# Scaling one half of each expert output block on VectorE, behind the weight splits

## The reference

```python
scores = sigmoid(x @ router_w)                     # 8 of 64 experts for each token, in 4 of 8 groups
w = take_along_axis(scores, top_idx, 1)
w = w / sum(w) * 2.5
def block_fn(acc, inp):                            # blocks of 128 rows, all of one expert
    rows, wts, e = inp
    yb = (silu(x[rows] @ w1[e]) * (x[rows] @ w3[e])) @ w2[e] * wts[:, None]
    return acc.at[rows].add(yb), None
ffn = routed[:N] + (silu(x @ sw1) * (x @ sw3)) @ sw2
x = layernorm(2 ** 0.25 * x + ffn)
```

## Time and profile before

| | |
|---|---|
| median of three runs | 2590.1 us |
| the profiled execution's own time | 2590.1 us |
| its span | 2588.2 us |
| TensorE clock granted, mean over the span | 0.933 |
| busy, of the span: PE, DVE, ACT, POOL | 88%, 48%, 34%, 24% |
| steps of the loop over experts between 1560 and 2515 us | 102 |

### The profile page before, as it was taken

How to read it: one execution, slowest core, us unless ns; L and a number is a source line. 1 busy time by engine, 2 the same in 40 slices (tenths; PEclk the granted TensorE clock), 3 DMA queues, 4 the chain that set the end, 5 groups by cost and what they waited for, 6 DMA issues and landing times.

```text
span 2588.2 us, 33805 instructions
## 1 busy us (share of the span) xinstructions
PE 2285.1 (88%) x8956; PEld 1519.7 (59%) x8957; DVE 1254.3 (48%) x2042; ACT 891.9 (34%) x1157; POOL 611.9 (24%) x412
## 2 busy tenths in 40 slices
PE   8994878999998999999891649999999999999980
PEld 3463554555554544444451538888887888888870
DVE  6365741333333411111337217767687676666647
ACT  1042103020101101000111117767686676666641
POOL 1000000212121100001000663444444444444432
PEclk9997969999999999999895769999999999999995
DMA  3101001000000011114522129999999999999954
GB/s 143 41 19 39 1 9 58 32 33 32 16 8 25 25 41 36 37 36 156 209 98 84 49 60 293 353 352 321 307 353 352 320 363 308 281 305 331 318 135 194
DMA packets 87770, 399.57 MB, mean 154 GB/s; under 512 B 15506, under 2 KB 15763, under 8 KB 61715
## 3 DMA queue, kind: packets, MB, share of 16 engines
q1 hardware_dynamic: 52546, 278.40, 28.2%
q0 software_dynamic: 35184, 120.67, 18.3%
HBM read 322.67 MB, written 75.18 MB: 154 GB/s over the span
## 4 chain that ended last, share of the span: by engine, by line
PE 61%; DVE 4%; DMA 3%; issue 2%; another core or an unknown queue 2%; ACT 1%; POOL 0%; POOLq 0%; ACTq 0%; SPq 0%; DVEq 0%
PE ps L621 33%; PE ps L1276 10%; PE ps L1284 5%; PE ps L615 4%; PE ps L576 3%; PE ps L1138 2%; DMA ffn_rows<-sig 1%; PE ps L647 1%; PE ps L1312 1%; DVE fr L956 1%; DMA wts<-in_experts 1%; PE ps L594 1%; DVE fst L958 0%; PE ps L587 0%
## 5 line engine op out<-in xcount | busy, mean ns | idle before, releaser
L621 PE MATMUL ps<-wts,xgT 128*128 x2616 | 628.6, 396 | 2.0 <-issue 1.9
L621 PEld LDWEIGHTS ps<-wts,xgT 128*128 128x128 f32 x2616 | 485.9, 189 | 102.4 <-issue 3.0
L882 DVE TENSOR_TENSOR wts<-wts (+1 forms) x195 | 444.2, 2291 | 139.6 <-ACT wts L697 78.1
L621 PE MATMUL ps<-wts,hTs 128*128 x1296 | 320.5, 394 | 23.4 <-issue 23.0
L1276 PE MATMUL ps<-xT,ring 128*128 128x512 f32 x768 | 334.7, 593 | 0.0
L540 POOL DMA_INDIRECT ffn_rows<-yo,sx x108 | 213.5, 1977 | 474.6 <-ACT yo L736 455.3
L1138 PE MATMUL ps<-xT,ring 128*128 128x512 f32 x704 | 311.4, 599 | 6.1 <-DMA ring<-in_w_in 6.1
L621 PEld LDWEIGHTS ps<-wts,hTs 128*128 128x128 f32 x1296 | 244.9, 189 | 80.6 <-issue 31.1
L692 ACT ACTIVATE wts<-wts (+1 forms) x130 | 242.9, 1929 | 41.3 <-DMA btab<-block_table 34.7
L1276 PEld LDWEIGHTS ps<-xT,ring 128*128 128x128 f32 x768 | 145.2, 190 | 178.9 <-issue 178.9
L522 POOL DMA_INDIRECT xg<-x_rows,ix x112 | 212.6, 1898 | 107.8 <-DVE ix L906 95.7
(11 more groups left out here) (358 smaller groups left out, 2301.1 us busy)
## 6 DMA issues: line engine op xcount, KB each, us to landing
wts<-in_experts SPq DMA_DIRECT2D x195, 1024.0 KB
ring<-in_w_in SPq DMA_DIRECT2D x52, 512.0 KB, 3.3
bring<-in_w_branch SPq DMA_DIRECT2D x24, 256.0 KB, 2.6
ffn_rows<-sig POOLq DMA_DIRECT2D x9, 512.0 KB
xT<-in_xT SPq DMA_DIRECT2D x4, 1024.0 KB, 9.3
wout<-in_w_out SPq DMA_DIRECT2D x1, 4096.0 KB, 12.2
N<-in_x SPq DMA_DIRECT2D x8, 512.0 KB, 3.6
x_rows<-N SPq DMA_DIRECT2D x8, 512.0 KB, 2.7
```

The costliest lines, as they stand in the source:

```text
L621: ins = mm(o, left(x), slot_cols(s, w, slice(c0, c0 + HALF)), start=first and n == 0, stop=last and n == 2)
L882: tt(w, w.bitcast(F32), hi, ALU.subtract).then_inc(done, 1)
```

## The change

The two halves of an output block no longer both belong to ACT. ACT scales the first (`ps[6]`) as before. DVE scales the second (`ps[7]`), as the last instruction of its step. The two copies `sx` and `wx`, with their wait for the add of two blocks before, move from ahead of the second part of the splits to behind it. The semaphores `e_y[0]`, `e_y[1]` become `e_ya`, `e_yd`, and PE waits for both ahead of the first half of its product.

```diff
@@ tail_pe
+                    pe.wait_ge(e_ya, i * 2 + u + ONE)
+                    pe.wait_ge(e_yd, i * 2 + u + ONE)
                     for h in range(2):
-                        pe.wait_ge(e_y[h], i * 2 + u + ONE)
@@ tail_act
                     act.wait_ge(e_Y, i * 2 + (u + 1) + ONE)
                     act.wait_ge(e_wx, i * 4 + (2 * u + 2))
-                    for h in range(2):
-                        A(yo[:, u, h * HALF:(h + 1) * HALF], ps[6 + h][:], ACT.Copy, scale=wx[:, u:u + 1]).then_inc(e_y[h], 1)
+                    A(yo[:, u, 0:HALF], ps[6][:], ACT.Copy, scale=wx[:, u:u + 1]).then_inc(e_ya, 1)
@@ tail_dve, block_step
                 hid(1 - u, i * 2 + (u + 2), i * 2 + u)
-                dve.wait_ge(e_sc[u], i * 16 + SC0[u])
-                dve.sem_inc(d_go, 1)
-                V.tensor_copy(sx[:, u:u + 1], slt[:, bass.ds(b, 1), 0:1].rearrange("p o w -> p (o w)")).then_inc(e_wx, 1)
-                V.tensor_copy(wx[:, u:u + 1], sltf[:, bass.ds(b, 1), 1:2].rearrange("p o w -> p (o w)")).then_inc(e_wx, 1)
                 with dve.If(first > 0):
                     split13(o, s, 1)
                 o, s, first = rows[u]
                 with dve.If(first > 0):
                     split2(o, s)
+                dve.wait_ge(e_sc[u], i * 16 + SC0[u])
+                dve.sem_inc(d_go, 1)
+                V.tensor_copy(sx[:, u:u + 1], slt[:, bass.ds(b, 1), 0:1].rearrange("p o w -> p (o w)")).then_inc(e_wx, 1)
+                V.tensor_copy(wx[:, u:u + 1], sltf[:, bass.ds(b, 1), 1:2].rearrange("p o w -> p (o w)")).then_inc(e_wx, 1)
+                dve.wait_ge(e_Y, i * 2 + (u + 1) + ONE)
+                dve.wait_ge(e_wx, i * 4 + (2 * u + 2))
+                ts(yo[:, u, HALF:D], ps[7][:], wx[:, u:u + 1], None, ALU.mult).then_inc(e_yd, 1)
```

More of the change, by code:

```diff
@@ L357, in build @@
         e_wx = sem("row_weight_ready")
-        e_y = [sem(f"output_half_scaled{i}") for i in range(2)]
+        e_ya = sem("output_half_act")
+        e_yd = sem("output_half_dve")
         e_sc = [sem(f"rows_adding{i}") for i in range(2)]
@@ L536, in add_rows @@
                 pool.wait_ge(e_sc[u], i * 16 + SC0[u])
-                pool.wait_ge(e_y[0], b + (1 + ONE))
-                pool.wait_ge(e_y[1], b + (1 + ONE))
+                pool.wait_ge(e_ya, b + (1 + ONE))
+                pool.wait_ge(e_yd, b + (1 + ONE))
                 pool.sem_inc(p_go, 1)
@@ L1374, in _ @@
             ch = Chain(act, s_act)
-            for one in (h_ev, *e_y, e_hTe):
+            for one in (h_ev, e_ya, e_hTe):
                 act.sem_inc(one, ONE)
@@ L1543, in _ @@
             ch = Chain(dve, s_dve)
-            for one in (h_o, h_qF, g_mix, e_hTl, e_hm):
+            for one in (h_o, h_qF, g_mix, e_yd, e_hTl, e_hm):
                 dve.sem_inc(one, ONE)
```

## The result

| | before | after |
|---|---|---|
| median (lowest to highest) of four runs | 2590.5 us (2590.0 to 2591.1) | 2660.0 us (2656.0 to 2662.8) |
| profiled execution, its span | 2590.1, 2588.2 | 2654.1, 2652.0 |
| granted clock over the span | 0.933 | 0.934 |
| busy, of the span: PE, DVE, ACT, POOL | 88%, 48%, 34%, 24% | 87%, 50%, 31%, 20% |

The kernel became slower, by a ratio of 1.0267 [1.0249, 1.0285]: 69.5 us. The direction and the place were as forecast. The size was not: +18.6 was expected, and 2660.0 lies far outside the range of 2598 to 2626.

A forecast was written before the change was run, and what follows sets the result against it. PE was taken to bound the expert loop at 9.31 us a step. Stalls 21.2, clock 4.8, late weights -6.8 and ACT's shorter end -0.6 sum to +18.6 on 2590.1: 2608.7 us, range 2598 to 2626.

The forecast's parts named there:

- The bound: In the expert loop PE sets the pace, 9.31 us a step, with 1.45 us of slack for `hm`.
- The ring: ACT's scaling waits for `wx` behind DVE's splits, and DVE's `hm` waits for ACT: 11.57 us against PE's 9.31.
- Its legs: Stretches between ACT's scaling, `hm`, DVE's splits and the copies: 6.27 us to `hm`, 5.30 back to the scaling.
- a run: Consecutive loop steps that each bring a new expert; from n = 3 on it costs 0.9 + 2.26(n-3) us.
- no change: Rival: DVE runs ahead, so ACT finds `wx` early enough; -0.6 to +5 us, about 2592; chance 0.07.
- a gain: Rival: in the shared expert's blocks POOL's add comes about 0.6 us sooner, moving the scatters; 2582 us; chance 0.03.
- The ring is longer than its legs: Rival: DVE's second half pays its branches in full, PE's product also waits for low hidden; +35 us, 2625; chance 0.20.
- the walk: Step-by-step count of lateness and PE stalls through steps with new experts and those behind them; 21.2 us in all.
- y: Time from PE's start of a step to ACT's scaling: 0.28 us before, forecast to reach 4.64.
- POOL's gather behind it: The next gather stands behind POOL's add, which waits for both halves; taken up two steps later, so put at nothing.
- The clock: PE's granted clock falls behind the last stall in runs of four (two) and six: 3 x 1.6 = 4.8 us.
- The weights' credit: Late weights in the run of six and behind the run of five no longer paid on top: -6.8 us.

## Why the prediction was right in direction and wrong in size

**What held.** The bound: with the copies anywhere ahead of `split2` and nothing else changed, PE kept its rhythm (traced excess 7.5, and 6.9 before). The ring: ACT's scaling waits for `wx`, and DVE's `hm` for ACT. Its legs: scaling to `hm` over a `split13` 6.47 us measured (1635.15 to 1641.62) for 6.27, `hm` to scaling over both splits 4.97 for 5.30, DVE's scaling 0.75 for 0.68. From the third step of a run on the scaling came at most 4.51 us behind PE's transposes, for 4.64. The rivals of no change and of a gain fell. "The ring is longer than its legs" is the nearest of them, but for its reason it fell too: it lengthened the branches, and the leg from `hm` to the split was 0.33 (1622.40 to 1622.73), the low end of the forecast.

**The step that failed** is this one of the walk: "After the run a step with `split2` alone brings y back to 0.99 and one with nothing to 0.28." It let DVE's split in that step follow `hm` after 0.50. In fact the split needs ACT's high part of w2, which takes 1.92 us and begins only behind the silu, so that it started 2.09 behind `hm` (1630.61 to 1632.70). The number was there: the earlier trace rows give DVE 78.1 us of waiting for ACT's L697. The walk used nothing of it. It was idle time of an engine that is not the bound, until the change put what ACT waits for behind it. So y is left at 2.93 where 0.99 was forecast (1632.22 to 1635.15), and the next new expert's step meets it: 2.93 + 6.27 = 9.20 against 8.65 allowed. The first step of every run but the first lost 0.5 us or more by it, 35 of 36, and 21 of the runs are single experts. Taking the leg out returned 42 of the 69.5 us and left 22.0 us in the steps with all splits, where the walk had 21.2. That is no proof of the walk's sizes: it had seven stalls of 2.26, and there were four, of 1.92 to 1.94 by the brackets and 2.1 by the starts, with others added. In part that is a misreading: 0.66 us from `hm` to PE was read from one row as the least, but it is 0.46 or 0.47 in half of PE's waits for `hm`, those of every second step (1622.40 to 1622.87), so that in every second step 0.2 us more was allowed.

**A second cost that the forecast did not have**: behind a stall of PE its table loads stand open ahead of the next product. Moving them alone gave back 19 us.

**DVE's scaling** was put at nothing, and so was POOL's gather behind it; alone, DVE's half cost 10 to 14 us, and PE did wait for the gather in it, which the forecast had named as a sign of being wrong; in the changed kernel it did not. The scaling took 0.75 us on DVE, and ACT's share fell by 0.58.

**The clock**, forecast at 4.8 us. PE had four stalls of 1.92 to 1.94 us inside or behind long runs. Behind three of them the clock was 0.50 for a while; behind the one at 1812.40 it stayed 1.00. The rows of PE and of the windows (us, busy by engine, granted clock, DMA share, GB/s):

```profile
1812.40 0.41 PE L648 MATMUL ps<-ident,hm 128*128 128x128 f32 x2 [1.94 <-DVE hm L878]
...
1955.60 0.66 PE L648 MATMUL ps<-ident,hm 128*128 128x128 f32 x2 [1.94 <-DVE hm L878]
...
1978.30 0.41 PE L648 MATMUL ps<-ident,hm 128*128 128x128 f32 x2 [1.92 <-DVE hm L878]
...
2141.97 0.41 PE L648 MATMUL ps<-ident,hm 128*128 128x128 f32 x2 [1.94 <-DVE hm L878]
...
2144.03 8.59 PE L622 MATMUL ps<-wts,xgT 128*128 x24 [0.58 <-DVE wts L883]
```

```profile
1812.00:1816.00 4.00, 2.98 (x17) 2.31 (x18) 4.00 (x3) 1.06 (x1) 0.69 (x1) 1.00 1.04 307
1956.00:1958.00 2.00, 2.00 (x11) 1.92 (x10) 2.00 (x2) 0.27 (x1) 0.00 (x0) 0.50 1.06 303
1980.00:1982.00 2.00, 1.67 (x4) 1.39 (x5) 2.00 (x2) 0.00 (x0) 0.00 (x0) 0.50 1.04 311
2145.00:2147.00 2.00, 2.00 (x6) 1.57 (x5) 1.96 (x4) 0.71 (x2) 0.00 (x0) 0.50 1.00 369
```

What a fall cost depends on where it was. The one at 1955.60 lay inside the run of six: its step took 11.25 us, no more than its neighbours at full clock (11.46 ahead of it, 11.45 behind it), because the ring set the pace there, as the forecast said. The other two lay behind the runs of six and of five, in steps that took 11.55 and 13.21 us for the 10.41 of the same kind of step at 1812.40: 1.14 and 2.80, together 3.9. The forecast's 4.8 is near that by luck. It charged 1.6 each behind the run of six and the two runs of four. Behind the runs of four the clock stayed at 1.00 (one of them had no stall over 0.7 us), and behind the run of five, which it left out, stood the dearest fall, above the 2.0 that it took as the upper end of one. The rule of the Trainium skill, "TensorE: Matmul & The Clock Gate", section "Why this matters for your kernels", that only longer idle gaps need to be avoided, is not borne out here: at 1955.60 the transposes that ended an idle time of 1.94 us already ran slow (0.66 us for 0.41). At the two other places PE did its ten transposes at nearly the full clock first, and stood idle another 0.4 to 0.6 us ahead of its product; it did the same at 1812.40, where the clock did not fall.

**The weights' credit** of 6.8 held as far as it can be seen: in the changed kernel's loop ACT waits for no weights at all, for 6.6 us ahead of `split13` before, and its stall at 1955.60 is for `hm` behind the ring.

**What stays open**: what DVE's half costs by itself, beyond the gather. The listed waits of PE (29.0 + 16.4 + 1.3) are no measure of the loss: the ends of PE's matmuls are modelled, which hides part of a gap. In the single run above the two steps up to 1884.07 lost 1.8 us, and the brackets show 0.62 + 0.55. The starts account for all 75.1, as 36.4 + 34.0 + 4.7.

## What to carry to other kernels

Before moving what an engine waits for behind another instruction, list everything that this instruction waits for in every kind of step, not only in the fullest one: a wait that costs nothing today is a leg of the ring tomorrow, and the rarer, lighter step can be the slower way around. A reset between bursts ("the next light step absorbs it") is an assumption that carries the whole sum, and is to be checked on rows as carefully as the burst. When an engine that never waited begins to stall, look also at what its queue has to do behind the wait. A releaser that the profile names is a candidate; move the other candidate and see whether the wait goes. Add up losses from starts, not from idle times in brackets.

## What the runs showed of the hardware

- Table loads in PE's queue behind a wait cost nothing where PE does not stall (2591.0 and 2590.7 us) and 19 us over the loop where it does (2660.0 to 2641.2). In the changed kernel they show as 0.41 to 0.72 us of idle PE ahead of the next product, and as about 1.0 us by the starts.
- The granted clock fell to 0.50 behind stalls of 1.92 to 1.94 us at three of four places. One such fall cost 2.8 us in its step, one 1.1, and one, inside a ring that set the pace, nothing that can be seen.
- A 128x512 scaling out of PSUM took DVE 0.75 us and ACT 0.69.
- The kernel before takes 2575 us in two comparisons and 2591 in others. Every trace of a kernel of this case from the two has 100.7 to 100.8 us for the first six steps of the loop, in which POOL scatters the table of slots, and every other has 115.7 to 116.0, whichever kernel it is. The kernel before was traced only in the second state, and why there are two is not shown.
